# An encoder layer with 32 experts on Trainium2: one scatter per expert, a plain copy to the outputs, and weights in halves

## The reference

```python
g_sel = jnp.argmax(g_logits, axis=-1)                  # one of 4 groups of experts per token
top_val, top_loc = lax.top_k(e_in, TOP_K)              # two of its 8 experts
gates = jax.nn.softmax(top_val, axis=-1) * g_gate
...
hb = jax.nn.silu(xb @ w_e_gate[e]) * (xb @ w_e_up[e])
return (hb @ w_e_down[e]).astype(jnp.float32) * wts[:, None]
...
out = x + sum over the two experts of a token
```

## Time and profile before

| | us |
|---|---|
| median of 3 runs | 1237.26 |
| lowest, highest | 1234.95, 1241.39 |
| the profiled execution | 1237.07 |
| its span | 1235.0 |
| busy in the span: PE | 1044.8 (85%) |
| busy: DVE | 781.9 (63%) |
| busy: ACT | 475.3 (38%) |
| busy: POOL | 409.1 (33%) |

### The profile page before, as it was taken

The page is one execution under the profiler, slowest core; times in us unless marked ns, Lnnn a source line. Parts: engine busy times, 40 slices in busy tenths (PEclk is TensorE's granted clock), DMA queues, the critical chain, the costliest instruction groups (busy, mean ns, idle before and its releaser), DMA issues.

```text
span 1235.0 us, 14036 instructions
## 1 busy us (share of the span) xinstructions
PE 1044.8 (85%) x5029; PEld 825.6 (67%) x5029; DVE 781.9 (63%) x1259; ACT 475.3 (38%) x849; POOL 409.1 (33%) x406
## 2 busy tenths in 40 slices
PE   1878978988897899899978999875998898889895
PEld 1746766857676677787857777764776576566663
DVE  4425765877666676773245566656977676768682
ACT  4222334333233523431123333333665455565460
POOL 1203403321341222110011111013475656667573
PEclk9989988879898897989988999986999999999998
DMA  5132223112222412424030011654798988898861
GB/s 189 37 89 74 94 69 121 34 53 77 62 77 99 140 51 88 145 92 149 31 95 30 34 52 52 251 226 147 268 369 328 352 304 324 346 361 318 347 241 41
DMA packets 73509, 193.25 MB, mean 156 GB/s; under 512 B 25120, under 2 KB 31680, under 8 KB 61152
## 3 DMA queue, kind: packets, MB, share of 16 engines
q1 hardware_dynamic: 43264, 146.95, 33.0%
q0 software_dynamic: 27328, 39.56, 9.3%
q10 hardware_dynamic: 2848, 5.84, 1.2%
HBM read 185.97 MB, written 65.01 MB: 203 GB/s over the span
## 4 chain that ended last, share of the span: by engine, by line
PE 38%; DVE 17%; DMA 15%; issue 12%; POOL 12%; ACT 6%; ACTq 0%; SPq 0%; DVEq 0%; POOLq 0%
DMA pg<-partial_rows,idh 13%; PE bank L903 8%; PE bank L904 8%; PE bank L905 8%; PE bank L953 2%; POOL y_sample L2374 2%; POOL xg L2369 2%; POOL partial_rows L2374 2%; DVE pg L2071 2%; DVE x_sb L1774 1%; DVE xn L1708 1%; DVE Wl L1699 1%; PE bank L1157 1%; ACT dec L1524 1%; POOL y_prompt L2374 1%
## 5 line engine op out<-in xcount | busy, mean ns | idle before, releaser
L903 PE MATMUL bank<-Wh,hTh 128*128 128x512 f32 x384 | 162.0, 422 | 4.6 <-issue 4.6
L904 PE MATMUL bank<-Wl,hTh 128*128 128x512 f32 x384 | 156.6, 408 | 0.0
L905 PE MATMUL bank<-Wh,hTl 128*128 128x512 f32 x384 | 156.2, 407 | 0.0
L1681 DVE TENSOR_TENSOR egl<-egr,ghi 128x2048 fp32r<-128x2048 f32 x64 | 143.7, 2284 | 4.0 <-ACT ghi L1356 4.0
L1356 ACT ACTIVATE ghi<-egr 128x2048 fp32r<-128x2048 f32 x64 | 119.3, 1921 | 0.0
L903 PE MATMUL gu_ps<-ghi,xgH 128*128 128x512 f32 x256 | 106.5, 416 | 1.4 <-DVE xgL L2048 1.4
L904 PE MATMUL gu_ps<-egl,xgH 128*128 128x512 f32 x256 | 103.0, 402 | 0.0
L905 PE MATMUL gu_ps<-ghi,xgL 128*128 128x512 f32 x256 | 102.8, 402 | 0.0
L1699 DVE TENSOR_TENSOR Wl<-raw,Wh 128x1024 fp32r<-128x1024 f32 (+1 forms) x64 | 77.4, 1217 | 37.6 <-ACT Wh L1356 37.4
L2071 DVE SCALAR_TENSOR_TENSOR pg<-y_ps,gate_s,pg 128x1024 f32<-128x1024 f32 x32 | 41.0, 1283 | 87.4 <-DMA pg<-partial_rows,idh 76.0
L903 PEld LDWEIGHTS bank<-Wh,hTh 128*128 128x128 f32 x384 | 77.6, 202 | 22.4 <-issue 6.6
(11 more groups left out here) (316 smaller groups left out, 2339.5 us busy)
## 6 DMA issues: line engine op xcount, KB each, us to landing
egr<-w_e_gate SPq DMA_DIRECT2D x32, 1024.0 KB, 11.0
egr<-w_e_up SPq DMA_DIRECT2D x32, 1024.0 KB, 13.6
edr<-w_e_down SPq DMA_DIRECT2D x32, 1024.0 KB, 7.6
raw<-w_in SPq DMA_DIRECT2D x72, 256.0 KB, 2.9
raw<-w_xkv SPq DMA_DIRECT2D x16, 256.0 KB, 3.0
raw<-w_out SPq DMA_DIRECT2D x16, 256.0 KB, 3.3
raw<-mix_scratch SPq DMA_DIRECT2D x16, 256.0 KB, 3.3
partial_rows<-x_sb ACTq DMA_DIRECT2D x8, 512.0 KB, 2.6
```

The costliest lines, as they stand in the source:

```text
L903: pe.matmul(dst, ah, bh, start=first, stop=False)
L904: pe.matmul(dst, ah, bl, start=False, stop=False)
L905: return pe.matmul(dst, al, bh, start=False, stop=last)
L1681: tt(egl[n % 4][:, a, :, :], egr[n % 4][:, a, :, :], ghi[n % 2][:, a, :, :].bitcast(F32), ALU.subtract)\
```

## The change

1. `store_rows(n)` issues one scatter, of all rows of the expert, to `partial_rows` by `idh`. The flag `sec`, the table `idf` and their computation are gone; `r_ps` takes 3 parts instead of 4.
2. For the last four experts (n = 28 to 31) no row is stored to `partial_rows`. Instead SP copies `partial_rows` to the two outputs in eight transfers of 512 KB when all scatters of n up to 27 have landed (`copied`), and then POOL scatters the rows of the last four experts over them (`out_rows`), by `idp` and `ids`, which are now `idh` cut to each half, made by `half_rows` in DVE's round 3.
3. `gather_sums(n + 1)` stands in round n instead of `gather_sums(n)`, and waits for one scatter (`px_st`).
4. POOL no longer waits for `meta_done` ahead of its loop; DVE's `add_rows(0)` does.
5. `load_piece` moves each weight matrix by two transfers, each with half of a partition's 8192 bytes, so one contiguous piece is 4096 bytes. The waits count 32 instead of 16.

```diff
-                sp.dma_start(to, w.rearrange("(p k) n -> p k n", p=P)).then_inc(done, 16)
+                w = w.rearrange("(p k) n -> p k n", p=P)
+                half = to.shape[1] // 2
+                for h in range(2):
+                    r = slice(half * h, half * h + half)
+                    sp.dma_start(to[:, r, :], w[:, r, :]).then_inc(done, 16)
...
+            for j in range(4):
+                sp.wait_ge(px_st[j], 16 * (NE // 4 - 1))
+            for i in range(NT):
+                sp.dma_start(out[i // TPS][0][(i % TPS) * P:(i % TPS + 1) * P, :], px_dram[i * P:(i + 1) * P, :])\
+                    .then_inc(copied, 16)
...
             def add_rows(n):
                 e = expert(n)
+                if n == 0:
+                    dve.wait_ge(meta_done, 1)
...
-                link(ts(place4[:, :, :], rk[:, :, :], float(P), 64.0, ALU.is_ge, ALU.mult))
-                link(tt(place4[:, :, :], place4[:, :, :], eix[:, :, :].rearrange("p t c -> p c t"), ALU.add))
-                for c in range(2):
-                    ins = tt(sec[:, c, :], place4[:, c, :], place4[:, 1 - c, :], ALU.is_gt)
...
-                for a, v in enumerate([sec[:, :, :]] + [gsp[:, g, :, :] for g in range(3)]):
+                for a, v in enumerate([gsp[:, g, :, :] for g in range(3)]):
...
-                stt(idf[:, :], r_w[:, 0, :], 5000.0, hrow1[:, :], ALU.mult, ALU.add)
...
+            def half_rows():
+
+                ts(idp[:, :], hrow1[:, :], 0.0, None, ALU.add)
                 link(ts(hrow4[:, :], hrow1[:, :], float(T), 5000.0, ALU.is_lt, ALU.mult))
...
+                stt(ids[:, :], hrow4[:, :], -float(T), hrow1[:, :], ALU.add, ALU.add).then_inc(halves_done, 1)
...
             def gather_sums(n):
                 e = expert(n)
                 if n > 3:
-                    pool.wait_ge(out_st[n % 4], 48 * (n // 4))
+                    pool.wait_ge(px_st[n % 4], 16 * (n // 4))
...
-                done, rows_ = out_st[n % 4], pg[n % 4][:, :]
-                spread_rows(px_dram, idf[:, e:e + 1], rows_, last_row).then_inc(done, 16)
-                spread_rows(out[0][0], idp[:, e:e + 1], rows_, last_half).then_inc(done, 16)
-                spread_rows(out[1][0], ids[:, e:e + 1], rows_, last_half).then_inc(done, 16)
+                spread_rows(px_dram, idh[:, e:e + 1], pg[n % 4][:, :], last_row).then_inc(px_st[n % 4], 16)
+
+            def out_rows(n):
+                e = expert(n)
+                pool.wait_ge(ey_done, n + 1)
+                pool.wait_ge(copied, 16 * NT)
+                pool.wait_ge(halves_done, 1)
+                spread_rows(out[0][0], idp[:, e:e + 1], pg[n % 4][:, :], last_half).then_inc(out_st, 16)
+                spread_rows(out[1][0], ids[:, e:e + 1], pg[n % 4][:, :], last_half).then_inc(out_st, 16)
...
-            pool.wait_ge(meta_done, 1)
             for n in range(1, NE):
-                if n > 1:
+                if 1 < n < NE - 2:
                     store_rows(n - 2)
                 if n + 3 < NE:
                     gather_rows(n + 3)
-                if n > 3:
-                    gather_sums(n)
-            store_rows(NE - 2)
-            store_rows(NE - 1)
...
+                if 2 < n < NE - 1:
+                    gather_sums(n + 1)
+            for n in range(NE - 4, NE):
+                out_rows(n)
+            pool.wait_ge(out_st, 16 * 8)
```

More of the change, by code:

```diff
@@ L527, in encoder_layer @@
         pos = se("pos", [P, 4, 2, NT], "gain", 2048)
-        idv3 = se("idv3", [P, 2 * NT, 6, NO + 1], "sqb", 0, BF16)
-        o_idx = se("o_idx", [P, 5, NO + 1], "prob", 0)
-        o_w = se("o_w", [P, 6, NO + 1], "prob", 512)
-        fid = [se(f"fid{i}", [P, 1], "prob", 1024 + 32 * i, U32) for i in range(4)]
+        idv3 = se("idv3", [P, 2 * NT, 5, NO + 1], "sqb", 0, BF16)
+        o_idx = se("o_idx", [P, 4, NO + 1], "prob", 0)
+        o_w = se("o_w", [P, 5, NO + 1], "prob", 512)
+        fid = [se(f"fid{i}", [P, 1], "prob", 1024 + 32 * i, U32) for i in range(2)]
         anchor = se("anchor", [P, 1], "prob", 1024 + 32 * 4)
@@ L566, in encoder_layer @@
         ey_done = sem("ey_done")
-        out_st = [sem(f"out_st{i}") for i in range(4)]
+        px_st = [sem(f"px_st{i}") for i in range(4)]
+        copied = sem("copied")
+        out_st = sem("out_st")
         o_v = sem("o_v")
@@ L1289, in more_first @@
                 for j in range(2 * NT):
-                    last = pe.matmul(r_ps[:, 0:6 * (NO + 1)].rearrange("p (a b) -> p a b", a=6), oneh_p[:, j, :],
+                    last = pe.matmul(r_ps[:, 0:5 * (NO + 1)].rearrange("p (a b) -> p a b", a=5), oneh_p[:, j, :],
                                      idv3[:, j, :, :], start=j == 0, stop=j == 2 * NT - 1)
@@ L2147, in _ @@
                     counts()
+                if n == 3:
+                    half_rows()
             hidden_low(NE - 1)
@@ L2182, in more_first @@
                 w = NO + 1
-                link(dve.tensor_copy(o_w[:, :, :].rearrange("p a b -> p (a b)"), r_ps[:, 0:6 * w]))
-                place, tile_, second = (o_w[:, a, :] for a in range(3))
+                link(dve.tensor_copy(o_w[:, :, :].rearrange("p a b -> p (a b)"), r_ps[:, 0:5 * w]))
+                place, tile_ = (o_w[:, a, :] for a in range(2))
                 link(ts(o_idx[:, 0, :], place, 0.0, 5000.0, ALU.is_equal, ALU.mult))
@@ L2411, in _ @@
                     gather_rows(n + 3)
-                if n > 3:
-                    gather_sums(n)
-            store_rows(NE - 2)
-            store_rows(NE - 1)
-            for j in range(4):
-                pool.wait_ge(out_st[j], 48 * (NE // 4))
+                if 2 < n < NE - 1:
[3 more added lines that the diff above has]
+            pool.wait_ge(out_st, 16 * 8)
             def more_first():
+                for n in range(NE - 4, NE):
+                    store_rows(n)
                 pool.wait_ge(o_v, 1)
```

54 lines of the change are left out of this document (22 added, 32 removed).

## The result

The changed kernel takes 1250.38 us (median of 4 runs, 1247.74 to 1252.58), the kernel before beside it 1236.11 (1234.09 to 1241.39): ratio 1.0096, 95% interval 1.0064 to 1.0129. It is slower by 14 us, where 46 us less were forecast. The profiled execution took 1252.4 us, its span 1250.4.

A forecast was written before the change was run, and what follows sets the result against it. The prediction took the loop through the gather of `pg` as the bound, with DMA and PE close behind. From 1237.07 us, -46.4 (steady), -0.8 (experts 27 to 31), -1.3 (end), -0.5 (DVE) and +2.9 (copy) gave 1191 us, range 1181 to 1213.

The forecast's parts named there:

- The loop through the gather: Expert stage: addition, POOL's scatters and gather of `pg` set the pace; gathering one expert sooner removes 76 us of DVE waits.
- (b): Weight queue: 4096-byte pieces instead of 8192 change its time per expert by -0.3 to +0.3 us; taken as zero.
- packets at the small price: Rival: 4096-byte weight packets move at the 2048-byte rate, 19.8 GB/s per engine; 12.4 us per expert, 1248 us; chance 0.04.
- the sum of DMA: Expert stage before the change: 8.09 us of weight queue plus 2.28 of POOL's queue, 10.37 us per expert.
- the prediction's own sign of being wrong: Expert stage: the forecast called itself wrong if DMA needed over 10.6 us per expert.
- the prediction's bounds: Packets under 512 B cost 14 to 30 ns each; 240 fewer save 0.2 to 0.45 us per expert.
- the loads run about three experts ahead: Weight loads on SP: with this lead, three more issues per expert, 1.3 us, cost nothing.
- The copy: End: copying `partial_rows` to the outputs costs 0 to 8 us; landing taken 30 us after addition 27, for +2.9 us.
- The end: After the last addition POOL issues two scatters instead of three: -1.3 us.
- Three more issues per expert: SP: the added weight-load issues, 0.43 us each and 1.3 us per expert, cost nothing.
- The term of DVE's operations: DVE: eleven small operations leave the first two rounds, three come in at round 3; -0.5 us, bounds 0 and -2.2.
- the steady part: Experts 4 to 27: 23 periods of 9.9 us instead of 274.1 us in all, -46.4 us.

The follow-up runs named there:

- e1_whole: The changed kernel with each weight matrix moved by one whole transfer again (8192-byte pieces): 1233.48 us, ratio 0.9942 to the kernel before.
- e7: The changed kernel with its two transfers per weight matrix cut into partitions 0 to 63 and 64 to 127, 8192-byte pieces: 1424.56 us, ratio 1.1513.
- e5: The changed kernel with whole weight transfers and real rows spread over both halves of the partitions: 1208.71 us, ratio 0.9764.
- e2_before_halves: The kernel before with only the weights moved in halves (4096-byte pieces): 1248.56 us, ratio 1.0085.
- e6_inner: Control: the changed kernel with slots reordered only inside each half of the partitions: 1255.6 us, ratio 1.0143.
- e12_after_even_odd: The changed kernel with its two weight transfers cut into even and odd partitions, 8192-byte pieces, slots unchanged: 1235.74 us, ratio 0.997.
- e3: The changed kernel, weights still in halves, with real rows spread over both halves of the partitions: 1219.39 us, ratio 0.9826.
- e9: e5 with one transfer per weight matrix but in 4096-byte pieces: 1213.05 us, ratio 0.9763 to the kernel before.
- e10: e5 with two transfers per weight matrix, even and odd partitions, 8192-byte pieces: 1206.25 us, ratio 0.9721 to the kernel before.
- e11: e5 with four transfers per weight matrix in 2048-byte pieces: 1214.34 us, ratio 0.9774 to the kernel before.
- e4: The kernel before with only the real rows spread over both halves of the partitions: 1223.73 us, ratio 0.9858.
- e8: e5 without the copy to the outputs and the waits on it: 1208.88 us, ratio 0.9759 to the kernel before.

## Why the prediction was wrong

*The loop through the gather: right.* The 76 us of waits went, the transposes of `xg` no longer wait, the new wait on `px_st` has no row (in e1_whole it has one, of 65.5 us in 22 waits, and DVE's additions still don't wait for the gather). That POOL's queue set the pace before was true, but something else stood close behind it.

*First failed step: (b), the price of 4096-byte pieces, "I take zero".* It was taken from eleven microseconds in which 4096-byte rows ran at 25.2 GB/s beside weights at 26.3, on another queue and ahead of the expert stage. Under load the weights in halves run at 3.146 MB / (16 x 8.64 us) = 22.8 GB/s, against 24.3 before and 25.1 whole in e1: q1 takes 8.64 us instead of 8.09. My upper bound for the term was +0.3, it measured +0.55 against before and +0.8 against e1. The price is one under this load and no constant: in e7 pieces of 8192 bytes took 13.4 us of q1 per expert. The rival "packets at the small price" had the mechanism and the sign, and its 1248 is near the result, but not its price: it asked for 19.8 GB/s and put its point of decision at 20.8, and the kernel became slower at 22.8. That its number is near is luck: its 12.0 us per expert are 9.9 + 2.1, where 8.6 + 3.5 stand below.

*Second failed step: the sum of DMA, "together 10.37 us".* By the mean over 16 engines the changed kernel needs 8.64 + 2.06 = 10.7 us, just past the prediction's own sign of being wrong (10.6), and its period is 1.3 us above even that. Two queues' shares were added as if all 16 engines carried them evenly. Take the real part of POOL's queue as 1.85 us per expert (e5's q0 of 20.3% is 2.14 us, less 240 small packets at some 20 ns over 16 engines; the 20 ns are an estimate between the prediction's bounds, whose lower one comes out at 10 rather than 14 ns when its sum is redone). If it falls on eight engines, less the few rows above 64, the fuller half carries about 1.9 times that, 3.5 us. Then that half needs, per expert:

| | q1 | + 3.5 | period |
|---|---|---|---|
| before | 8.09 | 11.6 | 11.92 |
| changed kernel | 8.64 | 12.1 | 12.02 |
| e1_whole | 7.83 | 11.3 | 11.21 |
| e2_before_halves | 8.49 | 12.0 | 11.96 |
| e6_inner | 8.61 | 12.1 | 12.22 |
| e12_after_even_odd | 8.25 | 11.8 | 11.47 |

and with even load, where q1 and q0 simply add: e3 8.45 + 2.06 = 10.5 (10.82), e5 8.09 + 2.14 = 10.2 (10.36), e9 8.36 + 2.08 = 10.4 (10.62), e10 8.09 + 2.08 = 10.2 (10.23), e11 8.65 + 2.08 = 10.7 (10.62). All agree within 0.35 us. The one that doesn't is e4, 7.98 + 2.39 = 10.4 against 11.28: there the gather loop and not DMA sets the pace. So the kernel before was not 1.5 us above its next bound, as 10.37 had it, but, by this estimate, 0.3. This, not the pieces, is where most of the forecast gain went: e1 shows that the scatter part brings 7 us instead of 46. The warning was in the earlier trace rows: a window of 9.73 us whose DMA share of 0.97 I read as DMA keeping up. But q1 moved only 2.98 MB in that window, and an expert has 3.146: buffers filled ahead made up the rest, and DMA was not keeping up.

*Third: "the loads run about three experts ahead".* True of gate and up, with four buffers, not of `w_down` with three. The chain in order of time of the changed kernel shows one loop (start, duration, what):

```profile
1007.74 0.33 SPq L860
1008.11 15.28 DMA edr<-w_e_down
...
1024.80 0.98 ACT xgH L1366 x2
1025.77 1.81 ACT ghi L1366
1027.61 1.84 DVE egl L1691
...
1029.82 2.29 DVE egl L1691
1032.11 0.34 DVE ehb L2071
1032.49 0.50 PE hb_ps L1263 x2
...
1041.65 0.87 PE y_ps L1276 x2
1042.54 0.33 SPq L860
1042.91 16.90 DMA edr<-w_e_down
```

The load is released by the product of three experts before, lands after 15.3 us, and 19.5 us later, by way of ACT, DVE and PE, the product of its own expert releases the next: 34.8 us for three experts. At PE's pace of 9.73 the loop has 3 x 9.73 - 19.5 = 9.7 us for the landing. DMA at its bound stretches the landing, and here that surfaces as a wait of ACT, in order, with `ghi` queued behind `dhi`. Whether the loop adds anything to the bound of DMA itself wasn't tried (it would take a fourth buffer or another queue).

*The copy: on the right side.* I took +2.9 us. SP issued it at 1209.77, and POOL's scatters show (start, duration, what, idle before):

```profile
1227.14 1.02 POOL L2380 DMA_INDIRECT y_prompt<-pg,idp  x1 [16.72 <-issue]
...
1233.62 0.97 POOL L2380 DMA_INDIRECT y_sample<-pg,ids  x1 [0.30 <-issue]
1236.35 0.97 POOL L2380 DMA_INDIRECT y_prompt<-pg,idp  x1 [1.76 <-DVE pg L2083]
1237.63 0.97 POOL L2380 DMA_INDIRECT y_sample<-pg,ids  x1 [0.30 <-issue]
```

The 16.72 us that no engine ended are the wait for the copy, whose last semaphore step stands at 1226.3 in the trace. It held POOL until 1227, 28.5 us after addition 27 (I had 30), and six scatters were through before the last addition, because these four experts took 36.2 us and not 33.2. e8 shows the same zero beside e5.

*The end.* The -1.3 came: from the last addition to the last scatter it is 2.84 us, before 4.11. But from the last scatter's start to the end of the span it is 1250.4 - 1237.63 = 12.8 us; before it was 1235.0 - 1225.73 = 9.3. e8 has 1208.9 - 1196.14 = 12.8 too, so the copy isn't the cause. The trace has the place: the last scatter lands 2.6 us after its start in both kernels, and behind it POOL executes a closing DRAIN of 8.89 us, where it was 5.22 before. It is 8.89 in each of the eleven profiles with the scatter part of the change and 5.22 in e2 and e4, without it. Why it grew stays open.

*SP and DVE.* Three more issues per expert cost nothing, as forecast: e10 has them and is as quick as e5. The term of DVE's operations (-0.5) is below what these runs can tell. The fit that the prediction takes from the Trainium skill ("DMA: Bandwidth & Descriptors", Anatomy of one DMA) is given there for DMAs that GpSimd issues, and the weights are issued by SP; its estimate of 19.2 against 13.2 us is for another path, and no term hung on it.

In sum, from the 1191 to the 1252.4 us of the profiled execution: the steady part was to be 23 x 9.9 and was 23 x 12.02, +48.8 us; 27 to 31 took 36.2 instead of 33.2, +3.0; the end 3.5, the copy 2.9 less, and about 1 us lies in the first rounds; 8.0 us are the first addition, at 881.83 instead of 873.86. The other profiles have it between 872.5 (e12) and 883.3 (e7), both with the change in, and at 882.0 in e4, which leaves both parts of the change out. That speaks for a difference from run to run ahead of the experts and against the change as its cause; this term is no failed step of the prediction.

In one sentence: DMA in the expert stage was taken as 10.0 us per expert, 8.1 for the weights and 1.9 for POOL, and needed about 12.1 on its fuller half: 8.6 measured for the weights, because 4096-byte pieces have a price, and an estimated 3.5 for POOL, whose real rows half of the engines carried.

## What to carry to other kernels

Before a forecast that takes DMA as "the next bound", ask which engines carry the bytes: gathers and scatters with empty slots should have their real rows spread over both halves of the partitions (here 2.5% on the changed kernel and 1.4% on the one before, for one line), and the fuller half is the bound, not the mean. The steps of a transfer's semaphore tell: two groups of eight are the sign. Where DMA is the bound, cut a transfer by even and odd partitions if it has to be cut, not by columns and never into the upper and the lower half. e5_whole_spread and e10_even_odd, at 1208.7 and 1206.3 us, are 2.4% and 2.8% below the kernel before (the interval of e5 reaches down to 1.8%). With the load even the scatter part of the change brings some 12 to 15 us (e4 to e5), against 7 with it uneven, and nowhere near the 46: PE and DMA stand too close behind the loop.

## What the runs showed of the hardware

A mean share of 0.90 for 16 DMA engines went with a full half: in the changed kernel, at 0.90, eight of the 16 parts of a gather landed over 2 us behind the others, and with the real rows spread (0.98) the same kernel was 31 us faster. Pieces of 4096 bytes cost 11 ns of engine time each more than pieces of 8192 bytes under load (24.3 to 23.5 GB/s per engine, e5 to e9), though rows of 4096 bytes on another queue had run at 25.2 in a quieter stretch. Two transfers of 64 neighbouring partitions fell to 14.6 GB/s per engine, two of 64 alternating ones kept 23.8 on the same kernel (24.3 with the rows spread). A DRAM-to-DRAM copy of 4.19 MB, issued just behind the last load, was through 16.6 us after its first issue, and after 16.0 to 18.7 us in the other kernels that have it. The DRAIN that closes POOL's program took 5.22 or 8.89 us, by the kernel and to the hundredth the same in each.
